# Eight reorderings in a three-block kernel: input load, hg gates, gla inputs, mlstm sums, stick-breaking inputs, ssd step sizes

## The reference, cut to what matters

```python
def reference(x, ...):
    x = first_block(x, ...)    # mixers hg, gla and mlstm
    x = second_block(x, ...)   # convolution and retention
    return third_block(x, ...) # rwkv, stick-breaking attention and ssd

# gated linear attention (hg and gla), head by head:
#   S_t = diag(exp(log_g_t)) S_{t-1} + k_t v_t^T ;  o_t = S_t^T q_t
# mlstm: the same with scalar gates i_t, f_t and a running maximum m_t;
#   q and k come out of a causal convolution of four taps and a Silu
# ssd: dt = softplus(dt_raw + dt_bias); decay exp(cumsum(-exp(a_log) dt));
#   x, B and C come out of a causal convolution of four taps and a Silu
```

## Time and profile before

| what | value |
|---|---|
| median of 3 runs | 4247.55 us (4244.5 to 4252.73) |
| the profiled execution, its own time | 4250.89 us |
| its span in the trace | 4249.1 us |
| mean granted clock of TensorE | 0.975 |
| TensorE busy | 4060.8 us of the span |

### The profile page before, as it was taken

One profiled execution on the slowest core, in us unless ns is written; L12 is line 12 of the kernel. 1 busy time (PEld: TensorE's weight loads), 2 busy tenths in 40 slices (PEclk: granted clock), 3 DMA queues, 4 the chain that ended last, 5 costly groups with the idle time before them and its releaser, 6 DMA issues. The chain is left out here.

```text
span 4249.1 us, 63997 instructions
## 1 busy us (share of the span) xinstructions
PE 4060.8 (96%) x26360; PEld 3274.0 (77%) x26360; DVE 2200.8 (52%) x2284; ACT 1314.8 (31%) x1589; POOL 987.3 (23%) x517
## 2 busy tenths in 40 slices
PE   7999998989999999999999999999999999998799
PEld 5888776868888888877767878888888777776677
DVE  7444554552323232379986554343434377766874
ACT  4333344121212121233212123131313355546612
POOL 2222222123232323200003333232323122221221
PEclk8999999999999999999999999999999999998899
DMA  3111224121212121122333211111111222226641
GB/s 128 60 59 59 98 89 163 56 87 51 71 45 70 50 70 45 58 71 75 122 136 120 89 67 56 52 57 50 59 49 59 87 80 79 79 76 218 218 184 60
DMA packets 114608, 361.14 MB, mean 85 GB/s; under 512 B 12916, under 2 KB 14596, under 8 KB 114248
## 3 DMA queue, kind: packets, MB, share of 16 engines
q1 hardware_dynamic: 82080, 292.56, 20.4%
q10 hardware_dynamic: 32296, 65.11, 4.1%
HBM read 263.03 MB, written 94.58 MB: 84 GB/s over the span
## 5 line engine op out<-in xcount | busy, mean ns | idle before, releaser
L409 POOL CAST b_w_hi<-b_w 128x1024 fp32r<-128x1024 f32 x233 | 266.6, 1144 | 2928.0 <-PE ps L505 2248.8
L505 PE MATMUL ps<-b_hi,b_w_hi 128*128 128x512 f32 x1872 | 750.5, 401 | 25.5 <-DVE b_w_lo L425 9.6
L505 PE MATMUL ps<-b_lo,b_w_hi 128*128 128x512 f32 x1872 | 731.9, 391 | 0.0
L505 PE MATMUL ps<-b_hi,b_w_lo 128*128 128x512 f32 x1872 | 731.3, 391 | 0.0
L411 POOL TENSOR_TENSOR b_w_lo<-b_w,b_w_hi 128x1024 fp32r<-128x1024 f32 x233 | 604.7, 2595 | 18.7
L505 PE MATMUL ps<-h_hT_hi,b_w_hi 128*128 128x512 f32 x1216 | 498.9, 410 | 7.4 <-DVE h_hT_lo L240 4.6
L505 PE MATMUL ps<-h_hT_lo,b_w_hi 128*128 128x512 f32 x1216 | 476.1, 392 | 0.0
L505 PE MATMUL ps<-h_hT_hi,b_w_lo 128*128 128x512 f32 x1216 | 476.0, 391 | 0.0
L505 PEld LDWEIGHTS ps<-b_hi,b_w_hi 128*128 128x128 f32 x1872 | 353.1, 189 | 113.9 <-issue 36.3
L505 PEld LDWEIGHTS ps<-b_lo,b_w_hi 128*128 128x128 f32 x1872 | 353.6, 189 | 79.3 <-issue 8.4
L505 PEld LDWEIGHTS ps<-b_hi,b_w_lo 128*128 128x128 f32 x1872 | 353.4, 189 | 74.2
(11 more groups left out here) (695 smaller groups left out, 6295.4 us busy)
## 6 DMA issues: line engine op xcount, KB each, us to landing
b_w<-in_w SPq DMA_DIRECT2D x277, 512.0 KB, 3.6
scratch_x_park<-xT SPq DMA_DIRECT2D x24, 512.0 KB, 3.9
conv_room<-scratch_gate_park SPq DMA_DIRECT2D x24, 512.0 KB, 4.6
xT<-scratch_x_park SPq DMA_DIRECT2D x16, 512.0 KB, 15.7
scratch_gate_park<-ret_fill_out ACTq DMA_DIRECT2D x32, 256.0 KB, 2.0
scratch_o_park<-ret_o ACTq DMA_DIRECT2D x16, 512.0 KB, 4.4
scratch_gate_park<-rw_fill_out ACTq DMA_DIRECT2D x32, 256.0 KB, 2.0
scratch_sb_park<-rw_fill_out ACTq DMA_DIRECT2D x32, 256.0 KB, 2.4
```

The costliest lines, as they stand in the source:

```text
L409: pool.tensor_copy(hi, w).then_inc(self.rounded, 1)
L505: ins = pe.matmul(out[:, t], w, y, start=start, stop=stop)
```

## The change

**Load.** The stage of constants is gone. `load_input` loads the identity first, then all eight tiles of x into eight buffers without waits; ACT's queue loads the other constants meanwhile.

```diff
-def load_input(core, x_dram):
...
-    ring = 4
...
+            sp.dma_start(core.ident[:, :], ident).then_inc(ident_loaded, 16)
             for c in range(NCH):
-                if c >= ring:
-                    sp.wait_ge(turned, c + 1 - ring)
-                    sp.wait_ge(squared, c + 1 - ring)
                 sp.dma_start(xin[:, c % ring, :], x_dram[c * P:(c + 1) * P, :]).then_inc(loaded[c % ring], 16)
...
-                if c >= ring:
-                    pe.wait_ge(kept, c + 1 - ring)
+                if c >= banks:
+                    pe.wait_ge(kept, c + 1 - banks)
...
+            for dst, src in others:
+                act.dma_start(dst, src).then_inc(others_loaded, 16)
...
+            act.wait_ge(others_loaded, 16 * len(others))
...
-        with Stage(nc, "consts") as st:
-            got = st.sem("consts_loaded")
-            block = st.block()
-
-            @block.sync
-            def _(sp):
-                for n in names:
-                    sp.dma_start(tiles[n][:, :], d["c_" + n]).then_inc(got, 16)
-                sp.dma_start(core.cols[:, :], d["cols"]).then_inc(got, 16)
-                sp.wait_ge(got, 16 * (len(names) + 1))
-        load_input(core, d["x"])
+        load_input(core, d["x"], d["c_ident"],
+                   [(core.cols[:, :], d["cols"])] + [(tiles[n][:, :], d["c_" + n]) for n in names[1:]])
```

```diff
-    def combine(self, dve, freed):
-
+    def read_out(self, dve, freed):
...
             dve.sem_inc(freed[n][0], freed[n][1])
+        step.ends(2)
+
+    def combine(self, dve):
+
+        gl, H = self.gl, self.H
+        step = Chain(dve, self.dve_step, 2)
...
+    BEFORE_GATES = 30
...
+            sp.wait_ge(S["unit_free"], 3)
+            for s in fill.stored:
+                sp.wait_ge(s, 16 * (1 + 2 * fill.n * 2 // fill.slots))
+            tiles = d["gla_park"].rearrange("(n p) t -> n p t", p=P)
+            for n, (tile, sem) in enumerate(((0, next_loaded[0]), (1, next_loaded[1]), (4, next_loaded[2]), (5, next_loaded[2]))):
+                sp.dma_start(next_in[:, n, :], tiles[tile]).then_inc(sem, 16)
...
-            gates.multiply(pe)
-            with pe.Fori(0, units) as u:
-                stream.multiply(pe, A[1], base, u, per)
-                pe.wait_ge(S["rooted"], u + 1)
+            def unit(u):
+                if isinstance(u, int):
+                    stream.multiply(pe, A[1], base, u, per, 0, BEFORE_GATES)
+                    gates.multiply(pe)
+                    stream.multiply(pe, A[1], base, u, per, BEFORE_GATES, 48)
...
+                    pe.wait_ge(S["rooted"], u)
...
+            unit(0)
+            with pe.Fori(1, units) as u:
+                unit(u)
+            fill.advance_next(pe, units, ahead)
...
-            gates.combine(dve, ((S["unit_free"], 1), (fill.kept, 2)))
+            gates.read_out(dve, ((S["unit_free"], 1), (fill.kept, 2)))
...
+            gates.combine(dve)
+            with dve.Fori(1, units) as u:
+                unit(u)
```

```diff
-        q, k, b = st.sb("q", [P, T]), st.sb("k", [P, T]), st.sb("b", [P, T])
+        q, k, att, b = inputs_now[:, 0, :], inputs_now[:, 1, :], inputs_now[:, 2:4, :], st.sb("b", [P, T])
...
-            inputs(tiles[0], tiles[1], [tiles[4], tiles[5]])
...
-                fill.advance(pe, u, begin, end // 2)
+                if u:
+                    fill.advance(pe, u, begin, end // 2)
...
-                fill.advance(pe, u, end // 2, end)
+                fill.advance(pe, u, end // 2 if u else ahead, end)
...
                     if sub:
-                        pe.wait_ge(S["rooted"], u * nsub + sub)
+                        pe.wait_ge(S["logged"], u * nsub + sub)
...
-            gates.finish(act, S["rows_exped"], S["rows_stored"])
             fill.begin(act)
             act.sem_inc(fill.kept, 2)
+            gates.finish(act, S["rows_exped"], S["rows_stored"])
...
-                    if sub:
-                        act.wait_ge(S["mean_done"], u * nsub + sub)
-                    act.activation(sq, A[sub], ACT.Square).then_inc(S["squared"], 1)
-                    if sub:
-                        act.activation(ks[:, 0, :], B, ACT.Ln, bias=core.const(NORM_EPS)).then_inc(S["logged"], 1)
-                        act.wait_ge(S["logged"], u * nsub + sub)
-                        act.activation(ks[:, 0, :], ks[:, 0, :], ACT.Exp, scale=-0.5).then_inc(S["rooted"], 1)
-                    else:
-                        fill.keep_parts(act, u, *span["out"])
-                fill.keep_parts(act, u, *span["mean0"])
-                act.wait_ge(S["mean_done"], u * nsub + nsub)
-                act.activation(ks[:, nsub - 1, :], B, ACT.Ln, bias=core.const(NORM_EPS)).then_inc(S["logged"], 1)
...
+                    act.activation(sq[sub], A[sub], ACT.Square).then_inc(S["squared"], 1)
+                fill.keep_parts(act, u, *span["out"])
+                for sub in range(nsub):
+                    act.wait_ge(S["mean_done"], u * nsub + (sub + 1))
+                    act.activation(ks[:, sub, :], B, ACT.Ln, bias=core.const(NORM_EPS)).then_inc(S["logged"], 1)
+                    act.wait_ge(S["logged"], u * nsub + (sub + 1))
+                    act.activation(ks[:, sub, :], ks[:, sub, :], ACT.Exp, scale=-0.5).then_inc(S["rooted"], 1)
+                    fill.keep_parts(act, u, *span[f"mean{sub}"])
...
-                       [14] + [5] * 8 + [4, 5, 5, 6, 22], core.xT[:, 4:8, :], gates)
+                       [18] + [5] * 6 + [4, 5, 4, 5, 5, 6, 19], ahead, core.xT[:, 4:8, :], gates)
```

```diff
-    PARTS = [12, 12, 10, 8, 8, 6, 8]
+    PARTS = [[16, 10, 12, 6, 8, 5, 7], [12, 12, 10, 8, 8, 6, 8]]
...
+        sq, vT, ktok, diag = brep, att, flat(state[:, :, :]), (diag[:, :, :], state[:, :, :])
...
-            for h in range(nsub * units):
-                sp.dma_start(y_ml[:, h, :], tile(8 + 6 * (h // 2) + h % 2)).then_inc(z_loaded[0], 16)
             for k in range(KD):
                 sp.wait_ge(S["y_cut"], k + 1)
                 sp.dma_start(x[:, k, :], x_park[k * P:(k + 1) * P, :]).then_inc(x_loaded[k], 16)
+                if k == 1:
+                    for h in range(nsub * units):
+                        sp.dma_start(y_ml[:, h, :], tile(8 + 6 * (h // 2) + h % 2)).then_inc(z_loaded[0], 16)
...
+            def add(i):
+                pool.wait_ge(x_loaded[i], 16)
+                for half in range(2):
+                    t = slice(half * 512, half * 512 + 512)
+                    pool.wait_ge(S["out_kept"], 2 * i + half + 3)
+                    pool.tensor_tensor(x[:, i, t], kept_out[:, half, :], x[:, i, t], ALU.add).then_inc(S["added"], 1)
+
             for n in range(KD):
                 stream.cut_tile(pool, base + stream.RING - 1 + n)
+                add(n)
...
+                    stream.multiply(pe, F, base + i, begin=n % 16 * 3, end=n % 16 * 3 + 3, free=(S["out_kept"], 2 * i + 1))
+
+            stream.multiply(pe, F, base, y_cut=S["y_cut"])
             pe.wait_ge(columns_loaded, 16)
...
-                pe.wait_ge(S["qk_ready"], u + 1)
+                pe.wait_ge(S["silu_done"], u * 2 + 2)
...
+            def keep(u, n):
+                i, half = u * tiles + n // 2, n % 2
+                act.wait_ge(stream.done, 4 * (base + i) + 2 * (half + 1))
+                if i:
+                    act.wait_ge(S["added"], 2 * (i - 1) + half + 1)
+                act.activation(kept_out[:, half, :], F[:, half * 512:half * 512 + 512], ACT.Copy).then_inc(S["out_kept"], 1)
...
+                keep(u, 2)
...
+                keep(u, 3)
+                keep(u, 4)
...
-                    dve.tensor_tensor(a, a, chunks(A[sub]), ALU.mult).then_inc(S["att_ready"], 1)
+                    dve.scalar_tensor_tensor(a, chunks(A[sub]), 64 ** -0.5, a, ALU.mult, ALU.mult).then_inc(S["att_ready"], 1)
...
-                step(dve.tensor_tensor(q[:, :], q[:, :], qdec[:, :], ALU.mult))
-                add(u, 2)
-                add(u, 3)
-
+                step(dve.scalar_tensor_tensor(q[:, :], q[:, :], 64 ** -0.5, qdec[:, :], ALU.mult, ALU.mult))
```

```diff
-            for n, (dst, sem) in enumerate(((q[:, :], q_loaded), (k[:, :], k_loaded), (vT[:, :], v_loaded))):
-                load(dst, sem, n * P)
...
+            sp.wait_ge(S["out_done"], units)
+            for s in fill.stored:
+                sp.wait_ge(s, 16 + 32 * fill.n // fill.slots)
+            for n, sem in enumerate(next_loaded):
+                sp.dma_start(next_in[:, n, :], sb_park[n * P:(n + 1) * P, :]).then_inc(sem, 16)
             sp.wait_ge(S["unit_free"], units + 1)
             sp.dma_start(y_park[(units - 1) * P:units * P, :], yo).then_inc(S["y_stored"], 16)
...
+            act.wait_ge(conv_done, 1)
+            act.activation(bt[:, :], bt[:, :], ACT.Silu, bias=core.col("ssd_cb", KD)).then_inc(activated, 1)
             act.wait_ge(stream.done, 4 * (base + 3))
             act.activation(pre[:, 1, 3:3 + T], pair(core, 2), ACT.Copy).then_inc(evacuated, 1)
-            act.wait_ge(conv_done, 1)
```

(50 more changed lines are left out.)

111 lines of the change are left out of this document (59 added, 52 removed).

## The result

The median after the change is 4203.97 us (4202.76 to 4206.9, 4 runs) against 4246.02 us (4238.85 to 4252.73, 4 runs) of the kernel before on the same chip: a ratio of 0.9902, 95% interval 0.989 to 0.9914. The profiled execution has a span of 4205.0 us where before had 4249.1, so 44.1 us shorter, at a mean granted clock of 0.978 where before had 0.975. The prediction was 4213 us, range 4197 to 4230, faster with 0.94.

What follows compares the result with a forecast made beforehand. The prediction took TensorE, busy for 4060.8 of 4249.1 us, as the bound, so only its waits and lower clock could pay. Terms 5 + 11.5 + 2.5 + 6.5 + 4.5 + 4.5 = 34.5 off the median 4247.55 gave 4213 us, range 4197 to 4230.

Steps and rivals of the forecast that it cites:

- the rival without new waits: gla, mlstm and ssd: removed waits have no successors; 47 us gained, 4200 us, chance 0.15 (4192 to 4205).
- named successors: New waits expected: gla's memsets 4.8, its displaced copies 9 in all, mlstm's third weight tile about 6, ssd's C.
- hg (11.5, measured 12.0): hg gates: 30 matmuls ahead cover the 6.8 us wait and keep full clock; 11.5 us, bounds 9 and 12.6.
- Load (5, measured 6.5): Load of x: issued about 1 us into the program instead of 6.92; 5 us gained, bounds 4 and 7.
- the step that gave 0.5 back: Load: x and constants at 348 GB/s make the stage 18.8 us instead of 18.3.
- gla (2.5, measured 5.0): gla: 4.1 at the start and 7.7 of waits gained, 9 of new waits; net 2.5 us, bounds -1 and 8.
- the 0.8 a unit: gla: last of three new waits from displaced ACT copies, estimated at 2.2, 1.5 and 0.8 us a unit.
- mlstm (6.5, measured 5.8): mlstm: 13.7 us gained, less about 6 for the third weight tile and 1.3 at the end; bounds 1 and 13.
- the two rivals about GpSimd: mlstm: adds hold up VectorE, 21 us lost, 4234 (0.22 shared with waits in full); or cuts come late, 4256 (0.02).
- GpSimd's order: mlstm: each cut stands behind an add and ACT's copy, slack 3.7 us a tile; slower case 4256, chance 0.02.
- Stick-breaking (4.5, measured 6.6): Stick-breaking: early q, k and v remove 4.9 of 7.0 us of waiting; 4.5 us taken, bounds 3 and 6.
- ssd (4.5, measured 2.8): ssd: the 4.10 us wait for step sizes goes, then the end hangs on C; 4.5 us, bounds 0.8 and 10.

Runs made afterwards that it cites:

- experiment 2: The changed kernel without TensorE's wait for the two memsets ahead of turning v in gla's first unit: 4203.22 us, ratio 0.9896.
- experiment 7: The changed kernel with x loaded through a ring of four buffers and its waits again: 4201.29 us in one execution, first weight load 3.2 us later.
- experiment 8: The kernel before with only TensorE's first hg unit written out ahead of the loop: 4243.21 us in one execution, rwkv 748.45 us against 752.00.
- experiment 1: The changed kernel with mlstm's third weight tile loaded right behind the second tile of x: 4199.29 us, ratio 0.9889.
- experiment 9: The changed kernel with each GpSimd add of a finished half done three times (add, take off, add again): 4210.24 us, ratio 0.9922.
- experiment 4: The changed kernel with one part of gla's filler moved from behind level 4 to behind level 6: 4198.96 us, ratio 0.988.

## Why the prediction was right

The time lies 9 us under the forecast and inside its range, and the cause is in the main the forecast's. It falls by 1 us into the band of the rival without new waits, but that rival is not what happened: the waits of the earlier trace rows went, and their named successors came. The trace gives 9.6 us more than the forecast's 34.5: rwkv, gla, stick-breaking, load and hg gave 10.6 more than their terms, the stages without a term 1.4, and ssd and mlstm 2.4 less. Of this rwkv's 4.0 had no term at all, and some of the rest is the spread between traces, so how near the sum came is in part luck. Term by term:

**hg (11.5, measured 12.0).** Right in each part. The open question, whether 16-row matmuls keep 2.4 GHz, came out as yes in the profiled execution (3.69 us for eight, PEclk 1.00 behind). It is not so in every trace: in experiment 2 the same eight matmuls, reached without a wait, took 4.16, and the stretch behind them ran at about 1.2 GHz:

```profile
53.00:60.00 7.00, 7.00 (x16) 4.56 (x15) 6.55 (x7) 5.26 (x6) 0.00 (x0) 0.51 0.13 52
```

16 matmuls start there where the kernel after has 31. Over the traces of the kernels that keep this edit, the way from the norm to hg's first level is 77.6 to 80.9 us for the same instructions. Five of the nine lie at 79.3, where the gain is 10.3 instead of 11.9 (89.61 before). The scans behind unit 0 cost nothing: VectorE's wait of the earlier trace rows covered them, though only just. They end at 177.9, unit 1 starts on VectorE at 178.31, and no wait of PE for them appears.

**Load (5, measured 6.5).** Mis-sized: the early start gave 5.1 (the first square at 6.78 for 11.91), but the step that gave 0.5 back was wrong. It paced the stage by DMA at the 348 GB/s of the earlier trace rows, whereas ScalarE's squares pace it, and with eight buffers none of them waits for x, which gave 1.4 more. DMA itself was faster too, 392 to 408 GB/s from 4 to 14 us. The ring's worth was in the upper bound and in no term of the sum; experiment 7 puts it at 3.2. Part of the 6.5 is the pair of traces: the first weight load is at 18.73 to 19.24 in the nine traces with the new load, and experiment 8, with the load of before, has it at 24.54, so the gain is 5.3 to 6.5.

**gla (2.5, measured 5.0).** The 4.8 at the start of gla, 2.2 a unit at the last level and 1.5 at the keys came as estimated (4.7, 2.4, 1.5). The mis-sized part is the count: the keys waited in one unit, not two, and the 0.8 a unit did not come; why is not shown.

**mlstm (6.5, measured 5.8).** The third tile's wait was 5.5 for "about 6", and experiment 1 took it away by DMA order alone; the end lost 1.3, as forecast. Of the two rivals about GpSimd, neither reached PE: its waits for the chain in mlstm come to 0.3 us. Held-up VectorE is a fact (1285 to 2079 ns on the key taps), off the path with 16 adds and worth 2.7 us of waits with 48. The Trainium skill, SBUF — State Buffer, section Who interferes with whom, states that a VectorE instruction with two SBUF inputs contends with a GpSimd instruction that reads SBUF. The trace agrees: such instructions grew and the one that reads PSUM did not. The time that the rival gave, 4234, did not follow. GpSimd's order was no limit either: in experiment 9, 5.2 us more a tile made PE's waits on cuts 0.4 us longer.

**Stick-breaking (4.5, measured 6.6).** The wait's part is 7.0 - 2.3 = 4.7. The rest is the clock behind it, which the prediction put into the upper bound only. In five other traces with this edit the stage was 1.6 us longer (33.4 us, where this trace and three others have 31.8), so the 4.7 is the sure part.

**ssd (4.5, measured 2.8).** The wait of 4.1 went and C became the end, 3.3 us late. TensorE in `ssd_gates` after, answering to the earlier trace rows:

```profile
3776.18 1.95 PE L2835 MATMUL ps<-c_ident_sb,ssdgate_cs 16*128 16x16 f32 x16
3777.99 3.09 PE L2835 MATMUL ps<-c_ident_sb,ssdgate_dt 16*128 16x16 f32 x16
3780.93 3.57 PE L2835 MATMUL ps<-c_ident_sb,ssdgate_de 16*128 16x16 f32 x16
3784.43 1.97 PE L2841 MATMUL ps<-c_ident_sb,ssdgate_bt 128*128 128x128 f32 x8
3789.70 6.50 PE L2847 MATMUL ps<-ssds_ct,ssdgate_bt 64*128 64x128 f32 x32 [3.30 <-ACT ssds_ct L2873]
```

The first sixteen run at full clock, during the second it falls, and the third run at half. So the gain lies below the value taken, on the side of the lower bound. In experiment 4, which changes nothing here, all kept it:

```profile
3775.53 1.95 PE L2835 MATMUL ps<-c_ident_sb,ssdgate_cs 16*128 16x16 f32 x16
3777.34 1.93 PE L2835 MATMUL ps<-c_ident_sb,ssdgate_dt 16*128 16x16 f32 x16
3779.12 1.93 PE L2835 MATMUL ps<-c_ident_sb,ssdgate_de 16*128 16x16 f32 x16
```

and the stage was 2.6 us shorter. Of the eight traces that have this stage as changed, three keep the clock for nearly all of the columns and five lose it as here. Each is of another build, so whether the build or the execution decides is not shown; the size of this term hangs on it.

**rwkv (not forecast, measured 4.0).** The only gain with a cause that the prediction did not have; experiment 8 ties 3.6 of it to the written-out unit. The change writes out gla's two units on TensorE as well, which the extract of the diff leaves out; what that does alone was not tried.

## What to carry to other kernels

Take a wait away only together with the question what is late next, and price that from the rows: here the five named in gla and mlstm came within 0.5 us of their estimates. Two of them then went with one more move in the order of a queue or a list, and half of a third by leaving out a wait of TensorE. Ahead of small matmuls put big ones rather than a wait: at hg that took away 6.8 us of waiting and, from trace to trace, 1.9 to 5.2 us more at the clock behind it. This load stage was paced by ScalarE and not by DMA, so ask which engine takes in what is loaded before reckoning with DMA's rate. And before a few us are put down to an edit, look at what the stages without an edit do from trace to trace.

## What the runs showed of the hardware that was not expected

- TensorE can pause inside a run of ready matmuls of 64x128 with no releaser (2.4 us over rwkv before, one pause of 0.4 to 1.0 in each unit), and the pauses are gone in the trace of experiment 8, whose edit in another branch only moves where its instructions lie.
- Matmuls with 16 rows that follow full work keep 2.4 GHz in one trace and lose it in another, with the same instructions ahead of them: eight at L846 3.69 or 4.16 us, sixteen at L2835 1.93 or 3.57.
- In the load stage of the kernel after DMA moved 392 to 408 GB/s from 4 to 14 us, over the 348 of the earlier trace rows.
